# The two layer joints of a three-layer network: tile order of the last weight unit, place of the token sums, and three units in place of two at the start of the next layer

## The reference, cut to what matters

```python
h = _rmsnorm(x, pre_g) * (1 + scale) + shift       # scale, shift, gate: silu(c) @ mod_w + mod_b
proj = h @ w_in
y = mixing(proj) * silu(z)                          # z is a part of proj: the gates
x = x + gate * _rmsnorm(y @ w_out, post_g)          # layer 3: no norm of the output
```

## Time and profile before

| What | Value |
|---|---|
| Median of 3 runs | 2586.74 us (2583.52 to 2589.63) |
| The profiled execution's own time | 2586.77 us |
| Its span in the profile | 2584.8 us |
| TensorE busy, share of the span | 98% |
| VectorE, ScalarE, GpSimd | 62%, 37%, 4% |
| TensorE weight loads (beside matmuls) | 78% |
| Granted TensorE clock, mean | 0.984 of 2.4 GHz |
| Data moved | 390.57 MB, mean 151 GB/s |

### The profile page before, as it was taken

How to read it: one execution, slowest core, us unless ns; L and a number is a source line. 1 busy time by engine, 2 the same in 40 slices (tenths; PEclk the granted TensorE clock), 3 DMA queues, 4 the chain that set the end, 5 groups by cost and what they waited for, 6 DMA issues and landing times.

```text
span 2584.8 us, 29837 instructions
## 1 busy us (share of the span) xinstructions
PE 2527.9 (98%) x11859; PEld 2024.6 (78%) x11859; DVE 1609.6 (62%) x2424; ACT 963.5 (37%) x1529; POOL 104.5 (4%) x115
## 2 busy tenths in 40 slices
PE   7999999999999999999999998999999999999998
PEld 4789777777778887888888887888788777887786
DVE  4456666667776758676776767266465577665532
ACT  4232444434454333332334333355455433233311
POOL 0000000000001103000000112000000000000000
PEclk8999999999999989999999998999999999999999
DMA  9955433344425744666645753322222245532342
GB/s 349 337 176 181 129 109 112 122 130 131 131 90 171 242 149 156 203 199 204 208 154 180 244 186 134 94 86 82 76 88 82 81 150 176 172 98 81 134 143 73
DMA packets 292876, 390.57 MB, mean 151 GB/s; under 512 B 11698, under 2 KB 221234, under 8 KB 288898
## 3 DMA queue, kind: packets, MB, share of 16 engines
q1 hardware_dynamic: 286608, 354.79, 43.1%
q0 software_dynamic: 6128, 33.89, 3.4%
q10 hardware_dynamic: 2, 0.00, 0.0%
HBM read 371.85 MB, written 16.78 MB: 150 GB/s over the span
## 4 chain that ended last, share of the span: by engine, by line
PE 92%; DVE 3%; DMA 2%; ACT 1%; SPq 1%; issue 1%; POOL 0%; DVEq 0%; POOLq 0%; ACTq 0%
PE G L2007 77%; PE S L2007 6%; PE OB L2007 5%; PE TB L2010 2%; PE TB L2007 1%; DMA MORE<-in_ev_mod_w 1%; DMA MRAW<-in_ev_mod_w 1%; DVE Y L1516 0%; SPq L1053 0%; PE OB L2010 0%; DVE WLO L1516 0%; DMA LATE<-in_ev_mod_w 0%; DVE TT L1516 0%; DVE HLO L1522 0%; ACT SQ L1170 0%
## 5 line engine op out<-in xcount | busy, mean ns | idle before, releaser
L2007 PE MATMUL G<-HHI,WLO 128*128 128x512 f32 x2624 | 1030.9, 393 | 0.0
L2007 PE MATMUL G<-HHI,WHI 128*128 128x512 f32 x1976 | 820.1, 415 | 17.5 <-issue 10.8
L2007 PE MATMUL G<-HLO,WHI 128*128 128x512 f32 x1976 | 773.1, 391 | 0.0
L2007 PEld LDWEIGHTS G<-HHI,WLO 128*128 128x128 f32 x2624 | 494.5, 188 | 110.9
L1173 ACT ACTIVATE WHI<-RAW 128x1024 fp32r<-128x1024 f32 x282 | 297.6, 1055 | 616.5 <-PE G L2007 563.3
L1516 DVE TENSOR_TENSOR WLO<-RAW,WHI 128x1024 fp32r<-128x1024 f32 x282 | 344.6, 1222 | 242.8 <-ACT WHI L1173 240.8
L2007 PEld LDWEIGHTS G<-HHI,WHI 128*128 128x128 f32 x1976 | 373.3, 189 | 100.2 <-issue 18.2
L2007 PEld LDWEIGHTS G<-HLO,WHI 128*128 128x128 f32 x1976 | 373.8, 189 | 79.8 <-issue 6.7
L1522 DVE SCALAR_TENSOR_TENSOR MACC<-MWIDE,SC,MACC 128x512 f32<-128x512 f32 x420 | 321.4, 765 | 42.9 <-DMA MWIDE<-in_w_ada 15.6
L2007 PE MATMUL G<-HHI,WHITA 128*128 128x512 f32 x544 | 224.9, 413 | 0.0
L2007 PE MATMUL G<-HLO,WHITA 128*128 128x512 f32 x544 | 214.6, 394 | 0.0
(11 more groups left out here) (310 smaller groups left out, 2848.5 us busy)
## 6 DMA issues: line engine op xcount, KB each, us to landing
RAW<-in_w_in SPq DMA_DIRECT2D x128, 512.0 KB, 3.7
MWIDE<-in_od_mod_w SPq DMA_DIRECT2D x96, 512.0 KB, 4.4
MWIDE<-in_w_ada SPq DMA_DIRECT2D x96, 512.0 KB, 4.7
RAW<-in_ev_w_in SPq DMA_DIRECT2D x80, 512.0 KB, 3.6
RAW<-in_od_w_in SPq DMA_DIRECT2D x64, 512.0 KB, 3.9
MWIDE<-in_ev_mod_w SPq DMA_DIRECT2D x32, 512.0 KB, 3.9
RAW<-in_ev_w_out SPq DMA_DIRECT2D x32, 512.0 KB, 3.5
RAW<-in_od_w_out SPq DMA_DIRECT2D x32, 512.0 KB, 3.5
```

What stands on the lines that cost most here:

```text
L2007: return e.o.matmul(o, l, r, start=start, stop=stop, skip_group_check=True)
```

## The change

- The last output unit goes through all four chunks for tile 14 first and then through all four for tile 15 (`gemm_last`), so tile 14 is ready half a unit (48 products) before the end.
- Tile 14 joins SUMS[0..2] (one more add on GpSimd, two more on VectorE), and the three sums over them are put at three places among tile 15's products (after steps 11, 13 and 14 of 0 to 15). Tile 14's own 24 records are gone; tile 15's stay.
- The new layer's first tile is worked on in another order: its scaling by TB stands inside "n_rstd", its add of x before the wait for the second root, SQ of tile 0 before anything of tile 1; the weight split stands behind the first pair; the gain's multiply moves from the end of "n_rstd" to the start of "o_rstd". A product with HHI waits for HHI alone, those behind it for HLO.
- Three units are begun together in place of two (`gemm_three`, 12 chunks): the two of before and the first gate unit, whose two tiles accumulate in OB and in the second half of S. With tiles 0 and 1, 36 products are made before tiles 2 and 3 are needed (12 before). The gate unit that stood behind is dropped, its silu starts behind the three, and `sb_task(0)` starts one unit earlier, before the values' unit. In layer 2 the four steps of `mods` that went with the dropped unit go with the last four chunks of the three.

The diff, cut:

```diff
+    G.append([OB, S[:, 512:1024]])
...
+    def three(w, *cols):
+        return [c for each in zip(*[weight(w, n) for n in cols]) for c in each]
...
-            units += [both(od_w, 0, 256)]
+            units += [three(od_w, 0, 256, 2048)]
...
-        units += [weight(od_w, 2048 + 512 * g), weight(od_w, 2048 + 512 * g + 256)]
+        units += [weight(od_w, 2048 + 512 * g)] if g else []
+        units += [weight(od_w, 2048 + 512 * g + 256)]
...
-            units += [both(w2, 0, 1024)]
+            units += [three(w2, 0, 1024, 3072)]
...
-        units += [weight(w2, 3072 + 256 * p)]
+        units += [weight(w2, 3072 + 256 * p)] if p else []
...
-        def gemm_dual(layer, tiles):
+        def gemm_three(layer, tiles):
             first = at["pair"] % 2
-            gated(0)
-            gated(1)
-            u = at["unit"]
+            for pair in range(3):
+                gated(pair)
+            pairs = (first, 1 - first, 2)
+            u, i0 = at["unit"], at["use"]
             at["unit"] += 1
             at["pair"] += 2
-            for c in range(8):
-                i = at["use"]
-                at["use"] += 1
-                while at["split"] <= i:
-                    split_next()
+            at["use"] += 12
+            next(tiles)
+            split_ahead(i0 - 1)
+            next(tiles)
+            for jj in range(2):
+                for uu in range(3):
+                    for nt in range(2):
+                        put("mm2", "h", layer, u, i0 + uu, uu, 0, nt, jj, pairs[uu])
+                    if jj:
+                        used(i0 + uu)
+                    if (jj, uu) != (1, 0):
+                        split_ahead(i0 + (uu if jj else 0))
+                    if (jj, uu) in ((0, 1), (1, 1)):
+                        next(tiles)
+            for c in range(3, 12):
+                i, uu = i0 + c, c % 3
                 for jj in range(2):
                     for nt in range(2):
-                        put("mm2", "h", layer, u, i, c % 2, c // 2 * 4, nt, jj, (first + c) % 2)
+                        put("mm2", "h", layer, u, i, uu, c // 3 * 4, nt, jj, pairs[uu])
                     if jj == 0:
                         split_ahead(i)
-                    next(tiles, None)
+                        next(tiles, None)
                 used(i)
-            for _ in tiles:
-                pass
+                if layer == 2 and c >= 8:
+                    reduce_pending()
+                    step([mods])
             return u, first
+
+        def gemm_last(layer):
+            pair = at["pair"] % 2
+            gated(pair)
+            u, i0 = at["unit"], at["use"]
+            at["unit"] += 1
+            at["pair"] += 1
+            at["use"] += 4
+            s = 0
+            for nt in range(2):
+                for c in range(4):
+                    for jj in range(2):
+                        put("mm", "y", layer, u, i0 + c, c, nt, jj, pair, c == 3)
+                        if jj == 0:
+                            if nt == 0:
+                                split_ahead(i0)
+                            elif c in (1, 2):
+                                split_ahead(i0 + c)
+                        step(background)
+                        if s == 7:
+                            put("o_copy", layer, 14, pair, 0, u, (u, 0))
+                        elif s == 8:
+                            put("o_more", layer, 14)
+                        elif s in (11, 13, 14):
+                            put("o_sum", layer, (11, 13, 14).index(s))
+                        s += 1
+                    if nt:
+                        used(i0 + c)
+                    elif c % 2:
+                        reduce_pending()
+                        step([mods])
+            return u, pair
...
-                u, pair = gemm("y", layer, uu == 7 and layer < 3)
+                if uu == 7 and layer < 3:
+                    u, pair = gemm_last(layer)
+                    finish(more)
+                    put("o_copy", layer, 15, pair, 1, u, (u, 1))
+                    put("o_more", layer, 15)
+                    break
+                u, pair = gemm("y", layer)
...
-                    if layer < 3 and uu == 7:
-                        put("o_more", layer, 14 + nt)
-                more = products(layer, (2 * uu, 2 * uu + 1), 3)
+                more = products(layer, (2 * uu, 2 * uu + 1), 3 if uu < 6 else 2)
...
-                if k == 13:
-                    for _ in range(7):
-                        yield
-                    put("o_sums", layer)
...
-                        if j < KT:
+                        if 1 < j < KT:
                             put("x_add", layer - 1, j)
                     if k % 4 == 2:
                         put("x_keep", layer, k // 4)
                     put("tile", layer, k, h_unit)
-                    if k > 2:
-                        yield
-                        yield
-
-            return gemm_dual(layer, tiles())
+                    yield
+
+            return gemm_three(layer, tiles())
...
+                silu(2, 0, 2, u)
...
-            for uu in range(2):
+            for uu in range(2) if g else (1,):
...
+                    if x:
+                        silu(3, 0, 2, u)
+                        tasks[0] = sb_task(0)
...
+            if n == 0:
+                continue
...
+        def x_scaled(layer, k):
+            e.wait_ge(p_xt, ("r1", layer))
+            e.wait_ge(a_sq, ("e", layer, k))
+            e.wait_ge(v_xy, (layer, k))
+            tt(Y[:, k, :], TB[:, :], Y[:, k, :], MUL).then_inc(*v_ux.up((layer, k, 1)))
+
+        def x_added(layer, k):
+            e.wait_ge(v_ux, (layer, k, 1))
+            e.wait_ge(back[k // 4], layer)
+            tt(Y[:, k, :], Y[:, k, :], XR[:, k, :], ADD).then_inc(*v_ux.up((layer, k, 2)))
...
+                e.wait_ge(v_mod, (11, 23)[layer - 1])
+                g = MOD[:, layer, 16:32]
+                gain = COL[:, 80:96] if layer == 1 else COL[:, 112:128]
+                stt(g, g, 1.0, gain, ADD, MUL).then_inc(*v_intro.up(("gain", layer + 1)))
...
+                x_scaled(layer - 1, 0)
...
+                if k == 0:
+                    x_added(layer - 1, 0)
...
+                    if j == 1:
+                        x_scaled(layer - 1, 1)
+                        x_added(layer - 1, 1)
...
+                    if kind == "h":
+                        e.wait_ge(a_h, ("t", layer, k))
+                    else:
+                        e.wait_ge(ready, key)
+                    if k == 0:
+                        e.wait_ge(*(gf[pair][nt] if pair < 2 else sf[1] if nt else ob))
+                    mm(G[pair][nt][:, :], wh[:, j, cols], hi, k == 0, False)
                     e.wait_ge(ready, key)
-                    if k == 0:
-                        e.wait_ge(*gf[pair][nt])
-                    t = split_mm(G[pair][nt][:, :], wh[:, j, cols], wl[:, j, cols], hi, lo, k == 0, k == 15)
+                    mm(G[pair][nt][:, :], wh[:, j, cols], lo, False, False)
+                    t = mm(G[pair][nt][:, :], wl[:, j, cols], hi, False, k == 15)
...
-            elif stage == "o_sums":
-                layer, = a
-                e.wait_ge(*ob)
-                e.wait_ge(*sf[1])
-                for x, (done, key) in enumerate(((g_sum, (layer, 13)), (v_xy, (layer, 13, "xy")),
-                                                 (v_xy, (layer, 13, "yy")))):
-                    e.wait_ge(done, key)
-                    token_sums(x, SUMS[x], x < 2)
+            elif stage == "o_sum":
+                layer, x = a
+                if x < 2:
+                    e.wait_ge(*(sf[1] if x else ob))
+                done, key = ((g_sum, (layer, 14)), (v_xy, (layer, 14, "xy")), (v_xy, (layer, 14, "yy")))[x]
+                e.wait_ge(done, key)
+                token_sums(x, SUMS[x], x < 2)
```

More of the change, by code:

```diff
@@ L293, in build @@
         first_chunk.append(first_chunk[-1] + len(u))
-    stick0, stick1 = first_chunk[third + 2], first_chunk[third + 16] + 4
+    stick0, stick1 = first_chunk[third + 1], first_chunk[third + 15] + 4
     fourths = range(3, len(chunks), 4)
@@ L352, in make_plan @@
         background = []
-        gates = [[], []]
+        gates = [[], [], []]
         at = {"load": 0, "split": 0, "use": 0, "done": 0, "unit": 0, "pair": 0, "heads": False, "hold": False, "extra": ()}
@@ L1104, in pool_program @@
                 layer, k, pair, nt, u, done = a
-                if layer < 3 and 0 < k < 14:
+                if layer < 3 and 0 < k < 15:
                     e.wait_ge(a_sqy, (layer, k))
@@ L1798, in dve_program @@
                 tt(t[:, :], Y[:, k, :], XR[:, k, :], MUL).then_inc(*v_xy.up((layer, k)))
-                if 0 < k < 14:
+                if 0 < k < 15:
                     e.wait_ge(a_sq, ("e", layer, k))
@@ L1838, in dve_program @@
                 stt(ROOT2, t, 1.5, y, ADD, MUL).then_inc(*v_rs.up((("n", layer), 4)))
-                e.wait_ge(v_mod, (11, 23)[layer - 2])
```

(47 more changed lines are left out.)

## The result

The changed kernel takes 2572.63 us (median of four runs, 2570.55 to 2573.62) against 2586.65 (four runs) before: a ratio of 0.9945, 95% interval 0.9928 to 0.9962, 14.0 us less. The profiled execution took 2572.38 us.

The account below looks back on a forecast made before the run. TensorE, busy 98%, was taken as the bound, with two joints losing 50.3 us. Per joint 2.7 + 5.2 + 7.3 - 0.2 + 2.1 = 17.1 remain, a gain of 16.1: 2570.6 us, range 2563.5 to 2579.5 (within 4 us: chance 0.55).

Parts of the forecast that it names:

- Sums among the products: Tile 14's sums, three groups among tile 15's products: 2.7 us per joint, no clock fall; bounds 0 and 1.5.
- E to T: Last output product's end (E) to last sum's end (T): 5.2 us per joint, 8.1 and 7.6 before.
- rival 3: At the joints, the clock holds to the last sum's end or returns at 3.3 us: 2566 us; chance 0.12.
- My lower bound, E + 3.6: Last sum's end at the joint if the last 16 records run at full clock, taking 1.6 us.
- T to the second product: Last sum's end to the new layer's steady flow, waiting for tile 0's HLO: about 7.3 us.
- the one ahead: New layer's first product, alone before the flow: starts 5.2 us behind the last sum, worth 0.2 us.
- Low clock at the restart: New layer's first products at half speed for 3.3 to 5.7 us: costs 2.1 us per joint.
- Rival 1: Clock stays low through the new layer's whole first group: 2577 us for one joint, 2583 for both; chance 0.12.
- No wait before the 37th: New layer's start: 36 products ready, so no wait for tiles 2 and 3; 1.9 us to spare.
- rival 2: In the twelve chunks, a new wait for HLO of tiles 2 and 3, or 6 and 7: 2578 us; chance 0.13.
- Sum: Both joints: 17.1 us each after the change, 34.2 together against 50.3 before; gain 16.1 us.
- VectorE in the twelve chunks: VectorE in the three units begun together: keeps up with the products, under 0.8 busy.
- `sb_task(0)`: Layer 3's first head task started a unit earlier: 0 us, bounds -1 and 2.

Follow-up runs that it names:

- a2: The changed kernel with the old last unit and the old place of the sums; 2580.74 us, ratio 0.9977.
- a1: The kernel before with only the last unit by column halves and tile 14 in the sums among the products; 2578.49 us, ratio 0.9961.
- c4: c2 with c3's delay of the first head task; 2571.71 us, ratio 0.9936.
- c3: The changed kernel with the first head task, `sb_task(0)`, started 8 steps later; 2570.00 us, ratio 0.9935.
- b1: The changed kernel with tile 0's HLO directly behind tile 1's scaling and tile 0's 18 products before tile 1's; 2570.06 us.
- c2: b1 with the third chunk's split in the last output unit, scaling of tiles 4, 5 behind tiles 2, 3, and useless products in the lulls; 2572.14 us.
- b2: The changed kernel with `sb_task(0)` started as late as before, behind the values' unit; 2578.88 us, ratio 0.9971.
- a3: The changed kernel with two units begun together and the gate unit behind, as before; 2581.03 us, ratio 0.9977.
- a4: The changed kernel with both tiles' scaling and adds and the split ahead of SQ, every product waiting for HLO; 2577.40 us.
- b3: The changed kernel with useless matmuls into OB in the joint's lull (5 and 6 around the second transposes, 8 behind the first product); 2571.37 us.

## Why the prediction was right, and which terms were off

The time, 2572.6, is 2.0 over the forecast of 2570.6 and inside its range, and the mechanism is the forecast's: with the last unit or the three units undone, their share of the gain goes (a2, a1). Step by step, per joint:

- **Sums among the products**: 2.7 taken, 2.75 measured. I took no fall of the clock among them, against 1.5 us for one. There is none at the 24 joints of the twelve kernels with the new last unit; with the old sums, all 24 records together, it stands at three of four (951.4 before, 952.5 and 1549.8 in a2).
- **E to T**: 5.2 taken, 3.9 and 4.4 measured. This term was mis-sized: "the fall stands in three of three cases", at E + 2.0 to 2.5. It came at E + 4.4 and 3.3: all sums of the first joint and 11 of the last 16 of the second ran at the full clock. That is the first half of rival 3, for which I had 0.12. Over the 24 joints with the new last unit the fall lies between E + 1.9 and 5.1, and only two (1.9 and 2.5, in c4 and c3) are as early as what I took from three cases. My lower bound, E + 3.6, was out of reach as well: 16 records take 1.96 us at the full clock and not 1.6, which gives the 3.9.
- **T to the second product**: 7.3 taken, 7.1 measured; the one ahead at 5.1 for 5.2. The chain built from single durations held to 0.2 us.
- **Low clock at the restart**: 2.1 taken. Without it the 48th product would start at the second's + 46 x 0.2275, T + 17.6; it does at 19.4 and 20.2, so 1.8 and 2.6. The clock was back 3.6 and 5.4 us after the second product, inside the 3.3 to 5.7 that I had, although I had read these from the first product, and from there it is 5.7 and 7.4 now. Rival 1 did not come.
- **No wait before the 37th**: right. The margin was as thin as the 1.9 us that I gave it: b1, whose flow starts 1.3 us earlier, waits there (0.3 us), which is rival 2 brought on by hand.
- **Sum**: 2.8 + 3.9 + 7.1 - 0.2 + 1.8 makes 15.4, the second joint 16.7 (0.2 is the product ahead), against 17.1 for each. From 50.3 that is a gain of 18.2; the joints taken directly gained 18.4, where I had 16.1.
- **VectorE in the twelve chunks**: I said under 0.8 busy. Its windows in the changed kernel, 0.78 and 0.73:

```profile
967.00:1033.00 66.00, 51.61 (x65) 0.97 0.52 175
1559.00:1625.00 66.00, 47.96 (x62) 0.96 0.50 162
```

The mean is right and tells little: c2 shows that in the first third the engine is the limit.

What was given back is in the terms that I had at nothing. **`sb_task(0)`** was taken at 0 with bounds -1 and 2. The net, 1.2 us longer with 1.3 us more waiting (2.4 against 1.1), lies inside; but the 0 had the wrong reason. I argued from little waiting in layer 3. b2 shows that dropping the unit without the early start costs some 9 us there (its second joint is 8.2 us shorter than before, and yet the stretch with it and layer 3's first half is 0.9 longer) and that the early start pays 7.9 of it back, at the price of a wait for V beside it, of which c3 takes 1.1 us away. Costs of "drop a unit" and "start the task sooner" should have stood as two terms.

The other 2.9 us came from code that is the same in both kernels: 1.3 ahead of layer 1's mark and 1.6 in the last stretch. In the last stretch TensorE has two lulls in both kernels, one of 3.7 us and one of 2.1 for HLO. The restart behind the second, each with the windows behind it, before the change and after (restarts at 2402.95 and 2387.11):

```profile
2402.95 0.50 PE L2007 MATMUL G<-HHI,WHI 128*128 128x512 f32 x1 [2.11 <-DVE HLO L1516]
```
```profile
2403.00:2406.00 3.00, 3.00 (x13) 1.00 0.02 5
```
```profile
2387.11 0.71 PE L2073 MATMUL G<-HHI,WHI 128*128 128x512 f32 x1 [2.10 <-DVE HLO L1570]
```
```profile
2388.00:2390.00 2.00, 2.00 (x6) 0.50 0.00 0
2390.00:2391.00 1.00, 1.00 (x4) 0.68 0.00 0
```

The same wait is followed by the full clock in one and by some 3.4 us of the low one in the other. The stretch is the same code in all kernels, and over the fourteen profiled executions it took between 0.1 us less and 2.9 us more than in that of before. It doesn't go by the edits in any way that I can see (0.0 in a1 and a3, 2.8 in a4 and b3, but -0.1 in c2, 0.1 in b2), so I take it for chance. That is not shown: there is one profiled execution of each kernel, and the three with two units (before, a1, a3) all lie at 0.0. Here the Trainium skill, "TensorE: Matmul & The Clock Gate", Part 1, has a rule that fits: the activity monitor runs freely, so the moment of the switch varies. The trace agrees, with -0.1 to 2.9 us for the same two lulls. What decides it in a given execution stays open.

The 1.3 us at the start look like the same thing. Up to 128 us the changed kernel is 0.25 ahead, from 140 on it is 1.3 behind. In between TensorE waits for modulation weights, 2.3 us before and 2.6 after, and the clock then is low for 3.4 us before and for 6.8 after; 3.4 us more at half speed can cost up to 1.7. TensorE's windows, before and after:

```profile
133.00:138.00 5.00, 5.00 (x37) 0.73 1.07 383
```
```profile
133.00:138.00 5.00, 5.00 (x34) 0.52 1.01 350
```

As a whole, then: the joints 2.3 better than forecast, 1.2 given back in layer 3 and 2.9 in unchanged code. The two errors have opposite signs, so that the total came out within 2.0 us is in part luck. These 2.0 us are also less than runs of one kernel scatter (3.1 us here), so only the terms, not the total, can be judged.

## What to carry to other kernels

At a point where one engine's chain must run alone (a norm over all channels), two edits help, and here their gains added up (8.7 and 6.5 us alone): finish one tile of the last unit early by going through it in column halves, so that only one tile is left to sum, and begin more units at once in banks that are spare there, so that the first pair of tiles carries more products than the next pair takes to make. Cover first, order second: bringing the first product forward without that cover moved the wait and made it longer (a3). And a dropped unit also takes away the steps that background work was hung on; start that work earlier by as much, and look at the next engine (here VectorE) before filling the lull further.

## What the hardware showed that was not expected

The granted clock (2.4 GHz, then 1.2) fell between 1.9 and 5.1 us after the last output product in kernels whose last unit and sums are the same, in twelve of 24 joints while the sums still ran. An early fall makes these slower: with the same instructions E to T is 3.9 us where they all ran at the full clock, 5.1 at c3's first joint (fall at E + 2.5) and 5.6 at c4's (E + 1.9). In b3 it fell at E + 4.4 although products of full size had just begun, and came back 3.4 us later while little but those ran. Keeping TensorE busy behind the sums thus did not hold the clock, but it made the low stretch shorter (3.4 us for 10.2), and this lay where nothing of use was slowed. Another moment for the fillers, before the sums, wasn't tried.
